# Two-block kernel in float32: transforms over tokens split into even and odd tokens, with mirrored frequencies made as sum and difference

## The reference, cut to what matters

```python
px = hx @ w_in[i]
...
four_x = fourier_mix(px[..., F0:H0], w_fourier[i])
hy_x = hyena_mix(px[..., H0:], w_hy_conv[i], b_hy_conv[i], hyena_filter(L, *hy_params), hy_bias[i])
mix_x = jnp.concatenate([attn_x, four_x, hy_x], axis=-1) @ w_out[i]

def fourier_mix(f, w):              # 256 channels in 4 groups of 64
    fg = f.reshape(B, L, 4, 64)
    y = jnp.fft.fft2(fg, axes=(1, 3), norm='ortho').real
    return y.reshape(B, L, 256) @ w

def hyena_longconv(u, filt, bias):  # 256 channels, n = 2 * L
    uf = jnp.fft.rfft(u, n=n, axis=1)
    kf = jnp.fft.rfft(filt, n=n, axis=0)
    y = jnp.fft.irfft(uf * kf[None], n=n, axis=1)[:, :L]
    return y + u * bias
```

## Time and profile before

| | |
|---|---|
| median of 3 runs | 2463.36 us (2462.01 to 2463.88) |
| profiled execution | 2455.66 us, its span 2453.9 us |
| granted TensorE clock, mean | 0.99 |
| busy: TensorE, VectorE, ScalarE, GpSimd | 94%, 66%, 41%, 29% |

### The profile page before, as it was taken

The page is one execution under the profiler, slowest core; times in us unless marked ns, Lnnn a source line. Parts: engine busy times, 40 slices in busy tenths (PEclk is TensorE's granted clock), DMA queues, the critical chain, the costliest instruction groups (busy, mean ns, idle before and its releaser), DMA issues.

```text
span 2453.9 us, 34867 instructions
## 1 busy us (share of the span) xinstructions
PE 2312.0 (94%) x11866; PEld 1799.3 (73%) x11866; DVE 1621.8 (66%) x2704; ACT 1016.1 (41%) x1662; POOL 708.9 (29%) x438
## 2 busy tenths in 40 slices
PE   8999889999788899979999999999899999999998
PEld 5766467666467699967666788888677667888886
DVE  8776588774587577455593576676564845776765
ACT  4344633346434466444262444432242524444421
POOL 3211043211133356622102333334221013333342
PEclk9999999999999999999999999999999999999999
DMA  5422224412144245542200243446521102343464
GB/s 210 167 75 69 69 104 174 148 52 69 52 175 126 81 146 181 180 162 69 95 27 11 93 153 132 152 155 228 187 89 69 53 1 95 137 149 135 145 235 142
DMA packets 81103, 293.96 MB, mean 120 GB/s; under 512 B 9009, under 2 KB 10450, under 8 KB 79028
## 3 DMA queue, kind: packets, MB, share of 16 engines
q1 hardware_dynamic: 80948, 292.03, 34.5%
HBM read 289.90 MB, written 2.10 MB: 119 GB/s over the span
## 4 chain that ended last, share of the span: by engine, by line
PE 52%; DVE 2%; issue 1%; ACT 1%; DVEq 0%; ACTq 0%
PE banks L1151 6%; PE banks L1157 6%; PE banks L1155 6%; PE banks L1173 3%; PE banks L1174 3%; PE banks L1180 3%; PE banks L882 3%; PE banks L883 3%; PE banks L887 3%; PE banks L1034 2%; PE banks L1053 2%; PE banks L1064 2%; PE banks L904 1%; PE banks L899 1%; PE banks L900 1%
## 5 line engine op out<-in xcount | busy, mean ns | idle before, releaser
L1480 ACT ACTIVATE wh_t<-ring 128x1024 fp32r<-128x1024 f32 x264 | 279.0, 1058 | 496.6 <-PE banks L1157 297.9
L1957 DVE TENSOR_TENSOR wl_t<-ring,wh_t 128x512 fp32r<-128x512 f32 x264 | 202.9, 769 | 286.2 <-ACT wh_t L1480 281.4
L2284 POOL TENSOR_TENSOR wl_t<-ring,wh_t 128x512 fp32r<-128x512 f32 x132 | 223.4, 1695 | 513.7 <-ACT wh_t L1480 492.2
L2322 POOL TENSOR_TENSOR wl_t<-ring,wh_t 128x512 fp32r<-128x512 f32 x132 | 236.6, 1793 | 419.8 <-ACT wh_t L1480 419.7
L2251 POOL TENSOR_TENSOR wl_t<-ring,wh_t 128x512 fp32r<-128x512 f32 x72 | 124.1, 1726 | 453.7 <-ACT wh_t L1238 437.1
L1151 PE MATMUL banks<-xh_t,wh_t 128*128 128x512 f32 (+1 forms) x960 | 203.0, 354 | 0.0
L1155 PE MATMUL banks<-xh_t,wl_t 128*128 128x512 f32 (+1 forms) x960 | 203.0, 354 | 0.0
L1157 PE MATMUL banks<-xl_t,wh_t 128*128 128x512 f32 (+1 forms) x960 | 203.0, 354 | 0.0
L1173 PE MATMUL banks<-gh_t,wh_t 128*128 128x512 f32 (+1 forms) x528 | 180.6, 354 | 1.0 <-ACT wh_t L1480 1.0
L1174 PE MATMUL banks<-gl_t,wh_t 128*128 128x512 f32 (+1 forms) x528 | 180.3, 354 | 0.0
L1155 PEld LDWEIGHTS banks<-xh_t,wl_t 128*128 128x128 f32 x960 | 161.4, 189 | 24.9
(11 more groups left out here) (378 smaller groups left out, 4616.7 us busy)
## 6 DMA issues: line engine op xcount, KB each, us to landing
ring<-w_d SPq DMA_DIRECT2D x338, 512.0 KB, 4.0
m_t<-wmod_d SPq DMA_DIRECT2D x160, 512.0 KB, 3.5
qh_t<-tables_d SPq DMA_DIRECT2D x6, 1024.0 KB, 5.0
m_t<-tables_d SPq DMA_DIRECT2D x6, 1024.0 KB, 7.9
par<-p_d SPq DMA_DIRECT2D x4, 696.0 KB, 6.3
x_t<-x_in_d SPq DMA_DIRECT2D x4, 512.0 KB, 7.5
big<-tables_d SPq DMA_DIRECT2D x2, 1024.0 KB
out_d<-x_t SPq DMA_DIRECT2D x4, 512.0 KB, 2.8
```

What stands on the lines that cost most here:

```text
L1480: nc.scalar.activation(WH[j % 2], slot2(j), ACT.Copy).then_inc(sm2["w2_hi"], 1)
L1957: nc.vector.tensor_tensor(WL[j % 2][:, 512:1024], slot2(j)[:, 512:1024], WH[j % 2][:, 512:1024].bitcast(F32), ALU.subtract).then_inc(sm2[" ...
L2284: pool.tensor_tensor(WL[j % 2][:, 0:512], slot2(j)[:, 0:512], WH[j % 2][:, 0:512].bitcast(F32), ALU.subtract).then_inc(sm2["w2_lo_a"], 1)
L2322: pool.tensor_tensor(WL[q % 2][:, 0:512], slot2(24 + q)[:, 0:512], WH[q % 2][:, 0:512].bitcast(F32), ALU.subtract).then_inc(sm2["w2_lo_a"], 1)
```

## The change

The tokens are put in the order even, then odd, and only the lower half of the frequencies gets a table. A transform then is two sums, over even tokens and over odd tokens; their sum is the value at a frequency, their difference that at the mirrored one (with signs that the code folds in). Each transform has half as many matmul columns.

- Spectrum: two blocks (one for the context), at j = 7 and 9. Even and odd parts in banks 6 and 7, the odd one copied by ScalarE (`odd_copy`), sum and difference by VectorE (`spectrum`).
- Fourier: even part in the bank of `acc`, odd part in banks 7 and 2; copy by ScalarE, sum and difference by VectorE (`fourier`).
- Forward transform: B / 2 blocks, four banks; odd copy by ScalarE between its copies of y (before c = 3 and c = 4); VectorE makes sum and difference (`PM`) and the products with the spectrum (`UM`, `CROSS`), twice as wide as before; GpSimd makes real and imaginary parts in two operations of 128x512; VectorE makes their sum and difference again (even and odd outputs), and TensorE takes them in the order of f.
- The bias product of y moves ahead of the transforms; y is completed in two strided halves.
- Blocks of tokens are read with a stride of two by `parity` in `fourier_in` and in the transposes of u.
- Tables have half the size. The second pair has a place of its own, is issued behind weight 11 and waits for no spectrum. The third is first needed by the inverse.
- One semaphore of the context's last part is gone, another takes its place.

```diff
-                TC=[TABC[:, i * n:(i + 1) * n] for i in range(b)], TS=[TABS[:, i * n:(i + 1) * n] for i in range(b)],
+                PM=[big[:, 14 * n + i * 1024:14 * n + (i + 1) * 1024] for i in range(b // 2)],
+                UM=[big[:, 18 * n + i * 1024:18 * n + (i + 1) * 1024] for i in range(b // 2)],
+                CROSS=[big[:, 22 * n + i * 1024:22 * n + (i + 1) * 1024] for i in range(b // 2)],
+                SPEC=[m_t[:, 2048 + i * 1024:3072 + i * 1024] for i in range(b // 2)],
+                TC=[TABC[:, i * h:(i + 1) * h] for i in range(b)], TS=[TABS[:, i * h:(i + 1) * h] for i in range(b)],
+                FC=[TABC[:, b * h + i * h:b * h + (i + 1) * h] for i in range(b)], FS=[TABS[:, b * h + i * h:b * h + (i + 1) * h] for i in range(b)],
+                IC=[TABC[:, b * h + i * n:b * h + (i + 1) * n] for i in range(b // 2)], IS=[TABS[:, b * h + i * n:b * h + (i + 1) * n] for i in range(b // 2)],
                 COS=cs_t[:, 0:n], SIN=cs_t[:, 512:512 + n], ROT=v3_t[:, 0:n], SQ=[prob_t[:, i * n:(i + 1) * n] for i in range(4)],
...
+
+            odd, k = divmod(b, blocks // 2)
+            return t.rearrange("p (t e) -> p e t", e=2)[:, odd, k * P:(k + 1) * P]
 
         def at2_of(is_ctx, l):
...
                 for i, dst in ((0, TABC), (1, TABS)):
-                    sp.dma_start(dst[:, 0:b * n], tab[i][:, 0:b * n]).then_inc(sm2["tables_f"], 16)
-                for j in range(R2, 14):
+                    sp.dma_start(dst[:, 0:half], tab[i][:, 0:half]).then_inc(sm2["tables_f"], 16)
+                for j in range(R2, 12):
                     weight(j)
-
-                sp.wait_ge(*at2("spec_ready", b))
                 for i, dst in ((2, TABC), (3, TABS)):
-                    sp.dma_start(dst[:, 0:b * n], tab[i][:, 0:b * n]).then_inc(sm2["tables_h"], 16)
-                for j in range(14, 14 + 4):
+                    sp.dma_start(dst[:, half:2 * half], tab[i][:, 0:half]).then_inc(sm2["tables_h"], 16)
+                for j in range(12, 14 + 4):
                     weight(j)
                 sp.wait_ge(*at2("acc2", 16))
                 for i, dst in ((4, TABC), (5, TABS)):
-                    sp.dma_start(dst[:, 0:b * n], tab[i][:, 0:b * n]).then_inc(tables_u[0 if is_ctx else 1], 16)
+                    sp.dma_start(dst[:, half:2 * half], tab[i][:, 0:half]).then_inc(tables_u[0 if is_ctx else 1], 16)
...
-                    if f >= 2:
-                        pe.wait_ge(*at2("spec_copied", f - 1))
-                    bank = ps[6 + f % 2]
-                    for b in range(B):
-                        pe.matmul(bank[:, 0:256], TC[b][:, f * P:(f + 1) * P], v["HP"][b], start=b == 0, stop=b == B - 1)
-                    for b in range(B):
-                        mm = pe.matmul(bank[:, 256:512], TS[b][:, f * P:(f + 1) * P], v["HM"][b], start=b == 0, stop=b == B - 1)
+                    if f >= 1:
+                        pe.wait_ge(*at2("spec_copied", f))
+                    for e in (1, 0):
+                        bank, half = ps[6 + e], range(e * B // 2, (e + 1) * B // 2)
+                        for b in half:
+                            pe.matmul(bank[:, 0:256], TC[b][:, f * P:(f + 1) * P], v["HP"][b], start=b == half[0], stop=b == half[-1])
+                        for b in half:
+                            mm = pe.matmul(bank[:, 256:512], TS[b][:, f * P:(f + 1) * P], v["HM"][b], start=b == half[0], stop=b == half[-1])
+                        if e:
+                            mm.then_inc(sm2["spec_ready"], 1)
```

```diff
                            7: [lambda: spectrum(0), lambda: head_sum(3)],
-                           8: [lambda: spectrum(1), lambda: head_turn(0), lambda: head_sum(4)],
-                           9: ([lambda: spectrum(2)] if B > 2 else []) + [filter_norm, lambda: head_turn(1)],
-                           10: ([lambda: spectrum(3)] if B > 2 else []) + [lambda: head_turn(2)],
+                           8: [lambda: head_turn(0), lambda: head_sum(4)],
+                           9: ([lambda: spectrum(1)] if B > 2 else []) + [filter_norm, lambda: head_turn(1)],
+                           10: [lambda: head_turn(2)],
```

```diff
-                    dst = acc(14 + i)
-                    for b in range(B):
-                        pe.matmul(dst, v["FG"][b][:, i * 256:i * 256 + P], TC[b], start=b == 0, stop=False)
-                        mm = pe.matmul(dst, v["FG"][b][:, i * 256 + P:(i + 1) * 256], TS[b], start=False, stop=b == B - 1)
+                    for e in (1, 0):
+                        dst, half = ps[(7, 2)[i]][:, 0:n // 2] if e else acc(14 + i, n // 2), range(e * B // 2, (e + 1) * B // 2)
+                        for b in half:
+                            pe.matmul(dst, v["FG"][b][:, i * 256:i * 256 + P], v["FC"][b], start=b == half[0], stop=False)
+                            mm = pe.matmul(dst, v["FG"][b][:, i * 256 + P:(i + 1) * 256], v["FS"][b], start=False, stop=b == half[-1])
+                        if e:
+                            mm.then_inc(sm2["four_ready"], 1)
                     mm.then_inc(sm2["acc2"], 1)
 
...
                 pe.wait_ge(*at2("ut_copied", B))
-                for f in range(B):
-                    bank = ps[5 + f % 2]
-                    if f >= 2:
-                        pe.wait_ge(*at2("us_mul", f - 1))
-                    for b in range(B):
-                        pe.matmul(bank[:, 0:256], TC[b][:, f * P:(f + 1) * P], v["UT"][b], start=b == 0, stop=b == B - 1)
-                    for b in range(B):
-                        mm = pe.matmul(bank[:, 256:512], TS[b][:, f * P:(f + 1) * P], v["UT"][b], start=b == 0, stop=b == B - 1)
+                for f in range(B // 2):
+                    for e in (1, 0):
+                        bank, half = ((ps[5], ps[6]), (ps[7], ps[2]))[f][e], range(e * B // 2, (e + 1) * B // 2)
+                        for b in half:
+                            pe.matmul(bank[:, 0:256], TC[b][:, f * P:(f + 1) * P], v["UT"][b], start=b == half[0], stop=b == half[-1])
+                        for b in half:
+                            mm = pe.matmul(bank[:, 256:512], TS[b][:, f * P:(f + 1) * P], v["UT"][b], start=b == half[0], stop=b == half[-1])
+                        if e:
+                            mm.then_inc(sm2["us_ready"], 1)
                     mm.then_inc(sm2["us_ready"], 1)
                 pe.wait_ge(*at2("oc2", len(tiles) // 2))
-                for i in range(2):
-                    dst = acc(18 + i)
-                    for f in range(B):
-                        pe.wait_ge(*at2("us_done", f + 1))
-                        pe.matmul(dst, v["YR"][f][:, i * P:(i + 1) * P], TC[f], start=f == 0, stop=False)
-                        mm = pe.matmul(dst, v["YI"][f][:, i * P:(i + 1) * P], TS[f], start=False, stop=f == B - 1)
-                    mm.then_inc(sm2["acc2"], 1)
+                pe.wait_ge(tables_u[0 if is_ctx else 1], 32 if is_ctx else l * 32 + 32)
+                outs = [(acc(18 + i)[:, 0:n // 2], ps[3 + i][:, 0:n // 2]) for i in range(2)]
+                for f in range(B // 2):
+                    pe.wait_ge(*at2("us_done", f + 1))
+                    for i in range(2):
+                        for e, dst in enumerate(outs[i]):
+                            cols = slice(e * n // 2, (e + 1) * n // 2)
+                            o = 512 * e + i * P
+                            pe.matmul(dst, v["UM"][f][:, o:o + P], v["IC"][f][:, cols], start=f == 0, stop=False)
+                            mm = pe.matmul(dst, v["UM"][f][:, o + 256:o + 256 + P], v["IS"][f][:, cols], start=False, stop=f == B // 2 - 1)
+                        if f == B // 2 - 1:
+                            mm.then_inc(sm2["acc2"], 1)
 
...
 
-                act.wait_ge(*at2("four_copied", B))
-                take(14, v["PX"][6])
+                for i in range(2):
+                    odd_copy(("four_ready", B + 1 + i), ps[(7, 2)[i]][:, 0:n // 2], v["PX"][6 + i][:, n // 2:n])
 
...
+                    if c in (3, 4) and c - 3 < B // 2:
+                        odd_copy(("us_ready", 2 * (c - 3) + 1), ps[(6, 2)[c - 3]][:], v["CROSS"][c - 3][:, 0:512])
                     if c >= 6:
...
+                def spectrum(f):
+
+                    dve.wait_ge(*at2("spec_ready", 2 * f + 2))
+                    dve.wait_ge(*at2("odd_copied", f + 1))
+                    odd = v["SPEC"][f][:, 512:1024]
+                    nc.vector.tensor_tensor(v["SPEC"][f][:, 0:512], ps[6][:], odd, ALU.add)
+                    nc.vector.tensor_tensor(odd, ps[6][:], odd, ALU.subtract).then_inc(sm2["spec_copied"], 1)
+
+                def fourier(i):
+
+                    dve.wait_ge(*at2("acc2", 14 + i + 1))
+                    dve.wait_ge(*at2("odd_copied", B // 2 + i + 1))
+                    even, odd = ps[i][:, 0:n // 2], v["PX"][6 + i][:, n // 2:n]
+                    nc.vector.tensor_tensor(v["PX"][6 + i][:, 0:n // 2], even, odd, ALU.add)
```

(38 more changed lines are left out.)

58 lines of the change are left out of this document (27 added, 31 removed).

## The result

The changed kernel takes **2420.65 us** (median of four, 2420.05 to 2428.23), the kernel before 2463.59 beside it (2462.01 to 2463.88): a ratio of **0.9834, 95% interval 0.9814 to 0.9854**. In four later executions (run 1) the changed kernel took 2419.4, 2419.8, 2424.2 and 2428.6 us; of 41 executions of the kernel before in all, 22 lie between 2453.3 and 2459.2 and 19 between 2460.9 and 2466.3. They come from four sets, each measured beside other runs, and the share of the higher times differs: 4 of 4, 1 of 9, 4 of 13 and 10 of 15.

A forecast was written before the change was run, and what follows sets the result against it. TensorE, busy 94% of the span, was taken as the bound; 2 x (6.9 + 6.9 + 2.8) - 4.05 = 29.2 us saved, so the median 2463.4 becomes 2434.2 us, range 2421 to 2446 (8 in 10).

The forecast's parts named there:

- Part 1: Filter spectrum at j = 7 to 10: two of four spectra go, VectorE's added work is covered; 6.9 us saved per x layer.
- Part 2: Fourier transform over tokens: 32 records of 256 columns instead of 512, VectorE's sums covered; 6.9 us saved per x layer.
- Part 3: The hyena's forward and inverse transforms: 2.8 us saved per x layer of the 13.8 us TensorE no longer works.
- step 3: Hyena, VectorE's f=0 work from 3.65: 3.9 us plus 1.2 for GpSimd's y_low(4), taking turns; done at 8.7.
- Bounds of 0.8 and 8.6 us: Hyena saving per x layer: 8.6 without sharing or slow clock, 0.8 with GpSimd at 1.8 us an operation.
- Context: Context layer: spectrum gains 1.0 us, Fourier loses 0.65, hyena loses 4.4; in all 4.05 us lost.
- The hyena's terms: Context's hyena: f=0 ready at 1.73, VectorE 3.9, GpSimd 2.5, VectorE 1.35 in a row, written as 9.9 us.
- Strided reads: Reading every second token in Fourier input, transposes and last additions: taken as 0, at most 4.5 us per x layer.
- Rival B: Strided operands cost their upper bound: 17.9 us saved, 2445.5 us; chance 0.12.
- Rival C: Clock stays low after the hyena's new gap, output product at half speed: slower, 11.4 us per stage; chance 0.04.
- Rival A: Hyena's engines don't get in each other's way and the clock holds: 42.8 us saved, 2420.6 us; chance 0.16.

The follow-up runs named there:

- run 1: The changed kernel measured once more, unedited: 2421.99 us (2419.43 to 2428.57).
- run 4: The changed kernel, but VectorE instead of GpSimd makes the hyena's real and imaginary parts: 2419.21 us.
- run 11: The changed kernel with 18 products of constants (16 in context) in TensorE's gap ahead of the inverse transform: 2417.65 us.
- run 5: The kernel before with 8 long-met waits (4 instructions) on VectorE ahead of the loop over the x layers: 2457.80 us.
- run 9: The kernel before with 24 long-met waits (12 instructions) on VectorE ahead of the loop over the x layers: 2452.77 us.
- run 8: The changed kernel, but Fourier input, hyena transposes and output sums take tokens in order, not every second one: 2423.91 us.
- run 6: The changed kernel with 120 long-met waits (60 instructions) on VectorE ahead of the x loop: 2424.41 us, two executions.
- run 10: The changed kernel with 232 long-met waits (116 instructions) on VectorE ahead of the x loop: 2431.65 us.

## Why the prediction was right, and where it fell short

- **Part 1**, 6.9 us forecast: 6.9 in either layer, no wait of TensorE ahead of product 8 or 10. VectorE's sums stood where the steps put them, 0.1 us off.
- **Part 2**, 6.9: 6.8 at the transform itself (13.83 and 7.00 us), 6.7 up to the forward transform (95.75 us between the two starts before, 89.03 after).
- **Part 3**, 2.8: output product 26.7 us after the forward transform forecast, 27.0 and 25.9 measured, 29.5 before: 2.5 and 3.6 us saved. Gap 9.6 forecast, 8.7 measured; f=0 at 16.4, measured 15.9. That VectorE and GpSimd take turns is as step 3 took it, but who waited is not: the 128x1024 product, expected longer than 1.22 us, took 1.23 both times, and GpSimd's two operations, expected near 1.24 us each, took 1.27, 2.28, 1.64 and 1.71. Bounds of 0.8 and 8.6 us hold both layers. (The lower bound's 1.8 us a GpSimd operation is not in the earlier trace rows, which has 1.695; with it 1.4 us or less would be left, not 1.1.) Of the 10 to 11 us per layer that TensorE no longer works here and that are not saved, run 4 gave 3 to 4 back (the hand-over, the sharing, and in layer 0 a shorter half clock), run 11 the clock's 1.6 to 2.7 (1.9 forecast).
- **Context**, 4.05 lost: 4.6. The hyena lost 3.7 (4.4 forecast), the spectrum gained 1.7 (1.0); part 2 lost 2.3 where 0.65 was forecast, of which about 1.7 is a new half-clock stretch of 3.4 us that the steps had not considered; 0.4 went ahead of the spectrum. The agreement is partly luck: against runs 5 and 9 the context lost 2.4, its hyena 2.0 (12.3 us there, 10.6 in the profile shown). The hyena's terms (1.73, 3.9, 2.5, 1.35) also add up to 9.5 us, not to the 9.9 written; 9.9 was measured.
- **Strided reads**, 0: right in time (run 8). Rival B falls. The prediction had named longer strided loads as a sign of being wrong; the sign came (207 ns for 141 in the transposes), the cost didn't. **Rival C** falls: in the changed kernel's profile full speed came back 3.4 us after TensorE's restart in layer 1 (records of 0.59 us from 1981.08 on), in layer 0 after some 5.3 us (run 1), and in no stage did the half clock behind the gap reach the output product. **Rival A** would have given 2420.6 us, and the median is there, but its conditions are not met: the sharing is in the rows (1.75 us for 0.68) and so is the clock. It is right in the number and wrong in the cause, by luck.
- **What was missing**: code position. The step that failed is the sum's, which took the rest of each layer as it was: 4.0 us of stall and 1.1 us of half clock behind it, in the kernel before, went away because 12 more VectorE instructions stand ahead of a loop. Set against run 9, the kernel before with nothing changed but that position, the changed kernel's lower-group execution is 2450.04 - 2419.43 = 30.6 us faster, 1.1 of it in the first block: 29.5, against 29.2 forecast. By parts: 16.2 and 17.3 us gained in the two x layers (16.6 forecast each), 2.4 lost in the context (4.05), 1.5 lost in half clock around layer 0's start, where nothing was forecast. So the sum is closer than its parts.
- **The reference**: the forecast subtracted from 2463.4, a median of the upper group, and the result's median is of the lower. From profile to profile (2455.66 and 2419.43) the gain is 36.2 us: 5.1 by the code's position, 2.1 in the first block, 29.0 the rest. The medians add 6.7, since 2463.59 stands 7.9 above the one profiled execution and 2420.65 1.2 above the other. So 42.9 = 29.0 + 5.1 + 2.1 + 6.7, and the last two are not the change's work. The 2.1 is clock in the first block; for the 6.7 there is no trace, and that it is the same clock is taken, not shown. What sets the group was not found. That its share went from 4 of 4 to 1 of 9 speaks against a plain toss for each execution; the later sets ran on three different chips, and whether the chip matters was not tested.

## What to carry to other kernels

Halving TensorE's work gains what the engines that prepare the next operand leave of it: here, over two layers, 27.3 us for the two (spectrum and Fourier) that ran beside other work, 6.1 for the two that have VectorE and GpSimd between them (forward and inverse). When a difference appears in a stretch that the edit doesn't touch, shift the code alone by a few instructions before explaining it: a 4 us stall at a loop's start belonged to neither kernel's work. Before using a median, find which group of times it stands in, by the granted clock of a stretch that the edit leaves alone, and take the kernel before again beside it: here its median moved by 8.7 us from one set to the next.

## What the runs showed of the hardware

- After the jump back to a loop's start, VectorE stood 4.0 to 4.2 us within the first dozen of the loop's instructions, where the kernel before enters the same loop at layer 0 with 0.20 us. 4 instructions more ahead of the loop moved the place, 12 and 72 removed it, 128 brought it back (runs 5, 9, 6, 10). Two packets of an instruction queue, 8 KB each, stood on either side of it.
- A VectorE operation of 128x512 with both inputs in SBUF took 1.75 us beside one of GpSimd, 0.68 without, and GpSimd's 1.5 to 2.3 instead of 1.27. With VectorE reading PSUM (0.68 us) neither was slower, and the one that began first kept its time (1.23 us for 128x1024 beside GpSimd's 2.28).
- TensorE kept at constants up to 0.9 us before its work was not slowed: 0.59 us a pair of records, where 8.7 us of idle time were followed by 1.06 for 3.4 us or more (granted clock 0.50), worth 1.6 to 2.7 us each time.
